# A new order for masks, roundings and norm steps in the last head group of a state-space stage

## What is computed

```python
def ssd_mixer(hn, w_in, conv_w, conv_b, dt_bias, a_log, d_skip, norm_g, w_out):
    proj = hn @ w_in
    z, xbc, dt_raw = jnp.split(proj, [SSD_INNER, SSD_INNER + SSD_XBC], axis=-1)
    xbc = jax.nn.silu(depthwise_conv_centered(xbc, conv_w, conv_b))
    ...
    y = bidir_scan(qc, kb, v_f, v_b, log_a[:, :, 0].reshape(grp), log_a[:, :, 1].reshape(grp))
    y = y + xh * d_skip ...
    y = y.reshape(bsz, s, SSD_INNER) * jax.nn.silu(z.astype(f32))
    yg = y.reshape(bsz, s, SSD_GROUPS, SSD_INNER // SSD_GROUPS)
    yg = yg * lax.rsqrt(jnp.mean(yg * yg, axis=-1, keepdims=True) + EPS)
    return (yg.reshape(bsz, s, SSD_INNER) * norm_g) @ w_out
```

## Time and profile before

| | |
|---|---|
| median of 3 runs | 1002.2 us (1001.03, 1002.2, 1005.2) |
| profiled execution | 1002.14 us, of which 1000.3 us are the span from first to last instruction |
| TensorE busy | 965.8 us, 97% of the span |
| GpSimd busy | 676.6 us, 68% |
| ScalarE busy | 605.4 us, 61% |
| VectorE busy | 471.4 us, 47% |

### The profile page before, as it was taken

How to read it: one execution, slowest core, us unless ns; L and a number is a source line. 1 busy time by engine, 2 the same in 40 slices (tenths; PEclk the granted TensorE clock), 3 DMA queues, 4 the chain that set the end, 5 groups by cost and what they waited for, 6 DMA issues and landing times. The chain is left out here.

```text
span 1000.3 us, 15875 instructions
## 1 busy us (share of the span) xinstructions
PE 965.8 (97%) x6093; PEld 847.5 (85%) x6093; DVE 471.4 (47%) x990; ACT 605.4 (61%) x1130; POOL 676.6 (68%) x538
## 2 busy tenths in 40 slices
PE   6999998999999999999998899999999999999998
PEld 5898787999999797888877699999997887788787
DVE  3744434544443645767844534353446222233652
ACT  7645656555545676877968654545557564775641
POOL 5986726766666785797778566656776963865574
PEclk9999999999999999999999899999999999999999
DMA  9774424766565556357446446555555537734321
GB/s 336 247 210 148 167 85 148 232 237 204 175 205 169 153 156 213 127 178 243 168 171 200 145 162 211 182 196 172 191 180 165 186 128 262 243 127 143 111 85 43
DMA packets 124952, 177.64 MB, mean 178 GB/s; under 512 B 13185, under 2 KB 86797, under 8 KB 124685
## 3 DMA queue, kind: packets, MB, share of 16 engines
q1 hardware_dynamic: 120701, 168.91, 51.4%
q10 hardware_dynamic: 4176, 7.71, 2.3%
HBM read 175.47 MB, written 5.24 MB: 181 GB/s over the span
## 5 line engine op out<-in xcount | busy, mean ns | idle before, releaser
L531 POOL TENSOR_TENSOR wlo<-raw,whi 128x512 fp32r<-128x512 f32 (+1 forms) x502 | 656.5, 1343 | 293.7 <-ACT whi L1218 277.9
L548 PE MATMUL PS<-Th,whi 128*128 128x256 f32 (+2 forms) x1000 | 286.7, 287 | 3.5 <-DVE Tl L1757 2.8
L550 PE MATMUL PS<-Th,wlo 128*128 128x256 f32 (+2 forms) x1000 | 283.4, 284 | 0.0
L549 PE MATMUL PS<-Tl,whi 128*128 128x256 f32 (+2 forms) x1000 | 283.4, 284 | 0.0
L1218 ACT ACTIVATE whi<-raw 128x1024 fp32r<-128x1024 f32 (+1 forms) x144 | 150.7, 1047 | 165.9 <-PE PS L550 123.7
L1832 DVE SCALAR_TENSOR_TENSOR arena<-PS,cols,arena 128x255 f32<-128x255 f32 (+1 forms) x272 | 118.6, 478 | 193.7 <-ACT arena L1351 166.8
L545 PE MATMUL PS<-whi,Th 128*128 128x512 f32 x480 | 194.4, 405 | 7.0 <-DVE Tl L1806 3.3
L548 PEld LDWEIGHTS PS<-Th,whi 128*128 128x128 f32 (+2 forms) x1000 | 192.2, 192 | 9.6 <-issue 5.6
L549 PEld LDWEIGHTS PS<-Tl,whi 128*128 128x128 f32 (+2 forms) x1000 | 192.2, 192 | 1.7 <-issue 0.7
L550 PEld LDWEIGHTS PS<-Th,wlo 128*128 128x128 f32 (+2 forms) x1000 | 192.0, 192 | 0.1
L547 PE MATMUL PS<-whi,Tl 128*128 128x512 f32 x480 | 189.0, 394 | 0.0
(11 more groups left out here) (242 smaller groups left out, 1037.8 us busy)
## 6 DMA issues: line engine op xcount, KB each, us to landing
raw<-in_ffn_w_up_dram SPq DMA_DIRECT2D x44, 1024.0 KB, 5.1
raw<-in_w_in_dram SPq DMA_DIRECT2D x23, 1024.0 KB, 5.4
raw<-in_ffn_w_down_dram SPq DMA_DIRECT2D x22, 1024.0 KB, 4.9
raw<-in_c_w_in_dram SPq DMA_DIRECT2D x16, 1024.0 KB, 5.3
raw<-in_ab_w_in_dram SPq DMA_DIRECT2D x14, 1024.0 KB, 6.9
raw<-in_c_w_out_dram SPq DMA_DIRECT2D x8, 1024.0 KB, 5.7
raw<-in_ab_w_out_dram SPq DMA_DIRECT2D x4, 1024.0 KB, 5.0
raw<-in_c_w_in_dram SPq DMA_DIRECT2D x8, 512.0 KB, 5.4
```

The costliest lines, as they stand in the source:

```text
L531: i = nc.gpsimd.tensor_tensor(lo_of(n)[:, c:e], raw[n % NRAW][:, c:e], hi_of(n)[:, c:e].bitcast(F32), ALU.subtract)
L548: mm(o, wh, ah, start=first, stop=False)
L549: mm(o, wh, al, start=False, stop=False)
L550: return mm(o, wl, ah, start=False, stop=last)
```

## The change

Four things, all for g = 3 (the last group) alone.

1. GpSimd masks pieces 0 to 3 ahead of the subtraction of O3, no longer ahead of that of O4.
2. ScalarE no longer rounds O1 ahead of the copies of the last gate block; it does so behind them, with O2.
3. ScalarE rounds O5 between E(3) and E(4), no longer between E(5) and E(6).
4. ScalarE does `last_root(1)` ahead of `last_hi(0)`, and VectorE `last_scale(1)` ahead of `last_lo(0)`.

No instruction is added or removed.

```diff
--- before.py
+++ after.py
@@ -403,7 +403,8 @@
         sums_before, kept_before = {}, {}
         for g in range(SG):
             b = slot_no[(("bc", g + 1), 0)] if g + 1 < SG else slot_no[("mo1", 0)]
-            for u, k, m in ((0, 5, 4), (2, 5, 4), (4, 7, 5), (6, 7, 5)):
+            first = 4 if g + 1 < SG else 3
+            for u, k, m in ((0, 5, first), (2, 5, first), (4, 7, 5), (6, 7, 5)):
                 sums_before.setdefault(b + k, []).append((g, u))
                 kept_before.setdefault(b + m, []).append(8 * g + u)
 
@@ -1528,7 +1529,8 @@
                         i = act.activation(o, crow[v % 4][:, k, :], ACT.Exp, bias=ncs[:, a:a + 1])
                     i.then_inc(*done("s_e", (g, u)))
 
-                high(b + 1)
+                if more:
+                    high(b + 1)
                 if g:
                     act.wait_ge(*at("w_used", slot_no[(("z", g), 1)]))
                     copy_block(("z", g), zt[g % 2], 0, func=ACT.Silu)
@@ -1556,6 +1558,8 @@
                 exps(3)
                 if more:
                     ssd_centre(g + 1, 1, False)
+                else:
+                    high(b + 5)
                 exps(4)
                 exps(5)
                 high(b + 5)
@@ -1568,8 +1572,8 @@
                     last_root(0)
                     load_gpost(2)
                     high(b + 7)
+                    last_root(1)
                     last_hi(0)
-                    last_root(1)
                     last_hi(1)
 
             def last_root(c):
@@ -2159,8 +2163,8 @@
             ssd_conv(0, 1)
             for g in range(SG):
                 ssd(g)
+            last_scale(1)
             last_lo(0)
-            last_scale(1)
             last_lo(1)
             post_norm(2, "ffn1", 0)
             ffn(1)
```

## The result

| | before | changed |
|---|---|---|
| median | 1002.2 us | 997.0 us |
| profiled execution | 1002.14 us | 995.63 us |
| its span | 1000.3 us | 993.7 us |
| ratio of the times | | 0.9938 (95%: 0.992 to 0.9956) |

The kernel is 0.62% faster, 5.2 us by the medians and 6.5 us by the two profiled executions. The forecast was 997.5 us, 4.7 less than before.

The account below looks back on a forecast made before the run. TensorE, busy 97% of the span, was taken as the bound, so only its last-group gaps could be won. 5.28 us out and 0.6 back in gave 4.7 us: 1002.14 to 997.4, put at 997.5; range 994.8 to 1000.6.

Parts of the forecast that it names:

- The sum: Last group, to O6's first product: 5.28 us of gaps out, 0.6 back in, 4.7 us gained.
- The three shifts: Chain to `masked(2)`: gate copies earlier worth 1.25 us, masks 1.85, O5's roundings 1.9.
- the six gaps: TensorE, last group: 1.25 ahead of O0, 0.51 in `tile_diag(0)`, 1.49 and 0.46 in `tile_diag(1)`, 0.88 and 0.69 at the turns.
- the new wait: TensorE ahead of O6, waiting for `last_lo(0)`, which the swap puts later: about 0.6 us.
- the overlap: TensorE products start 0.16 us before the previous one ends, so a gap is worth its bracket plus 0.16 us.
- The bracket ahead of O0: TensorE's 1.09 us wait for ScalarE's gate copies; part 2 removes it whole, worth 1.25 us.
- I count it evenly: Half-clock stretch behind the following norm, 6.2 us long, some 3.1 us lost: could get shorter or longer, so no net effect.
- no change: Whole kernel: a difference under 0.5%, 5.0 us, down to 997.2 us; the forecast lay just inside, chance 0.59.
- a sign of being wrong: Profile after: among others, a half-clock stretch whose length differs by more than 1 us.
- GpSimd as the bound: Rival, chance 0.18: ties behind mask 7 become TensorE waits at O5 and O7 of 0.6 to 2 us; 998 to 1000.
- The slower rival: Chance 0.04: late rows hold masks 0 to 3 and O3's subtraction behind them on GpSimd; at 530 us, 1010.
- The exclusion: O1's subtraction: GpSimd and two-input VectorE operations exclude each other; later start gives GpSimd back about 0.4 us, TensorE nothing.

Follow-up runs that it names:

- the four variants: Changed kernel without the swap, ratio to before 0.9928; that with second last_turn inside O6, 0.9939; changed kernel with two extra idle products, 0.9934; both additions together, 0.993.
- part 2 alone: Kernel of before with only O1's roundings moved behind the last gate copies; 999.38 us in one execution.
- GpSimd late: Changed kernel with GpSimd doing the first piece of O5's subtraction two times more, 2.5 us of extra work; 997.55 us in one execution.
- the swap alone: Kernel of before with only part 4, the swap at the end; 1002.21 us in one execution, before on the same chip 1002.48.
- the turn inside O6: Changed kernel without the swap, second last_turn put behind O6's first six products on TensorE; median 997.0 us of six, ratio to before 0.9939.
- the idle products alone: Changed kernel with two more products on idle data in the norm ahead of the second feed-forward part; median 995.72 us of five, ratio to before 0.9934.
- the masks one slot earlier still: Changed kernel with masks 0 to 3 ahead of O2's subtraction instead of O3's; 995.78 us in one execution.

## Why the prediction was right, and what it missed

**The sum.** Each moment came out to 0.3 us but one, once the 0.35 us by which the changed kernel's trace is ahead at group 2's products is added: gate copies at 502.4 (502.65 said), masks 0 to 3 from 514.4 (515.1, which nothing hangs on), E(2) at 521.75 (521.8), O5's roundings over at 530.6 (530.6), `masked(2)` at 534.8 (534.8), mask 7 at 533.8 (533.6), the first turn at 542.4 (542.6), the second at 545.6 (545.8), O6 at 546.9 (546.9) with a wait of 0.65 (0.6). The three shifts were shown one by one. The swap cost 0.2 and 0.3 us, the lower end of the -0.3 to +0.3 said, so of the four parts three made the gain and the fourth took a little of it back.

Two terms of the sum were off and cancel. By segments of the two timelines the six gaps gave back 5.5 to 5.6 us where 5.28 was called the most that they could, and the new wait cost 0.8 to 0.9 (its bracket of 0.65 and the overlap, which the sum left out here) instead of 0.6. That they cancel follows from the chain: O6 starts when `last_lo(0)` is done, 12.13 us after `masked(2)` (12.1 said), however early TensorE gets there.

**A size that was part luck.** The bracket ahead of O0 counted 1.25 us. In the three other traces that have it, it is 0.67 to 0.74 instead of 1.09. So the typical worth of part 2 may be nearer 0.9, and the 4.7 of one pair of traces nearer 4.3 for the usual execution; that is an estimate from four traces.

**What failed** is the step "I count it evenly", on the clock, and with it the call of "no change" as the likeliest class (0.59 against 0.38; the ratio is 0.62% below one, though its interval reaches to 0.9956, inside the 0.5% called no change). The half-clock stretch did what the prediction had named as a sign of being wrong: it was 3.4 us shorter, more than 1. The step also had a wrong price. It put 6.2 us at 1.2 GHz at some 3.1 us lost, half of their length; measured, 6.8 us cost 2.4, and the halved stretch gave back 1.1 us instead of some 1.6.

Every execution reports its span and mean granted clock. For 17 of before, run beside the experiments, the mean span is 1000.7 us and the mean clock 0.9924, for the 8 of the changed kernel 994.3 us and 0.9956: 6.4 us apart. The two sets did not run beside each other, but the 20 executions of the four variants that ran beside the 17 of before stand at 0.994 to 0.998 as well, and those of before at 0.988 to 0.998. Eleven of before stand at 0.993, with 999.3 to 1001.2 us, mean 1000.3; two of the changed kernel stand at 0.993, with 995.1 and 995.2. At 0.998 there is one of each, 997.5 and 992.4. At an equal clock it is thus 5.1 us, or with the slope of a straight line through either set (592 us for the whole clock before and 488 after, so 1.6 to 1.9 us for 0.0032) 4.5 to 4.8. The rest, 1 to 2 us, goes with less time at the half clock. The two profiles say the same: 13.6 us of half clock before and 6.8 after, not counting the end of the span, and 1.7 us between them by the distances above.

**Is that the change's doing?** In the last group itself it can be: in two kernels that kept or made a long bracket there (1.31 and 0.23 in part 2 alone, 2.33 with GpSimd late) a half-clock stretch began within 0.5 us of the last bracket's end and cost 0.6 and 1.5 us more. The eight kernels without a bracket of over 1 us there show none. But before's own profile and the swap alone have the brackets of 1.34 and 1.35 and no such stretch, so a bracket makes it possible and not certain. That it accounts for the whole difference of the mean clock was not shown: the two profiles differ in stretches behind the norms, at 569 and 763 us, where no bracket changed. The Trainium skill (TensorE: Matmul & The Clock Gate, what is actually happening) says that the observation runs on by itself, untied to the program. These runs agree in that the same brackets have a stretch behind them in one trace and none in another; no run here shows the cause.

**The rivals.** GpSimd as the bound did not come, but by little: with the turn inside O6 it was there, 0.38 us at O7, and the trace with the idle products alone, whose last group is the changed kernel's, has a wait of 0.15 us for GpSimd ahead of O5. The slower rival had no foothold, since the masks could go one slot further without a loss. Some tenths of the 5.1 us at equal clock lie outside the last group; what they are stays open.

## What to carry to other kernels

When a chain of short waits crosses four engines, find the one moment that all later steps hang on (here `masked(2)`), and count each reordering as a shift of that moment; such shifts add, and the next wait behind them can be read from the old trace as a distance from it. A swap of two steps at the end of a chain can merely move a wait from one consumer to the next one, as here, where it cost 0.2 to 0.3 us; so price both consumers. And a gap of TensorE can be worth more than its length: before calling a gain too small to tell, compare executions at equal granted clock. The same holds for distances in single traces: measure them from the moment that the step under test hangs on, or a bracket ahead of it that differs by chance hides the effect, as in the swap alone.

## What the runs showed of the hardware

Every one of the twelve traces had stretches at 1.2 GHz, most of them 3.4 us long and two of 6.8, at places that changed from execution to execution (near 73, 157, 388, 541, 567, 763 and 904 us, and often at the very end). The one near 388 us was in ten of the twelve, no other in more than seven. A stretch of 3.4 us cost 0.5 us near 764 us, 0.6 in the second `tile_diag` of part 2 alone, 1.1 or 1.3 behind the third norm, and 1.5 in the middle of O5 when GpSimd was late.

VectorE's two scalings between buffers in SBUF (line 2056 before, 2060 after, 128x512 each) took 0.88 us together with GpSimd idle, 1.33 us beside its masks, and 2.49 us beside its subtractions (shown above under the masks one slot earlier still); the eight subtractions in that trace took 10.40 us, while the eight of O1 and O2 in the changed kernel took 10.04. The Trainium skill (SBUF, State Buffer, the section on who interferes with whom) counts `tensor_scalar` among VectorE's operations that can take the ports shared with GpSimd, and whoever issues first then blocks the other for the whole instruction; these rows agree in that both engines were slower beside each other. The exclusion stood in the prediction for O1's subtraction: its eight pieces took 10.42 us beside VectorE's line 2072 and 10.04 in the changed kernel, where line 2076, the same operation, was over, the 0.4 us said there, and TensorE won nothing by it. The scalings before and after the change:

```profile
...
517.33 0.88 DVE L2056 TENSOR_SCALAR hn<-hn,st 128x512 f32<-128x512 f32 x2
...
```

```profile
...
515.62 1.33 DVE L2060 TENSOR_SCALAR hn<-hn,st 128x512 f32<-128x512 f32 x2
...
```
